# Head means of the delta rule: from one float32 product to two float32r products, with the sums split by ScalarE and VectorE and the products one unit of weights later

## The chip, the core and the metric

The kernel runs on one core of one Trainium2 chip. The metric is the device time of the whole kernel in microseconds (us). One launch computes both layers of the block.

## The reference, cut to what matters

Each of two layers has four mixers side by side. The change touches the end of the first, the gated delta rule:

```python
oa = gated_delta_chunked(qa, ka, va, beta, g).transpose(0, 2, 1, 3)      # 4 heads of 128, 512 tokens
oa = rmsnorm(oa, gdn_norm) * jax.nn.silu(gdn_z.reshape(B, S, GDN_HEADS, GDN_DV).astype(f32))
y_a = oa.reshape(B, S, -1).astype(x.dtype) @ w_br_a
...
g_a, g_b, g_c, g_d = jnp.split(jax.nn.sigmoid(gates), N_BRANCH, axis=-1)
mixed = (g_a * y_a + g_b * y_b + g_c * y_c + g_d * y_d) @ w_o
```

For each head and token, `rmsnorm` needs the mean over the head's 128 values of their squares. The kernel leaves the scale of the queries out of the recurrence, so the epsilon of the norm is multiplied by the queries' own sum of squares, which is added to the squares before the mean is taken.

## The kernel before, in words

Activations lie transposed: 128 channels on the partitions, 512 tokens along the row. A head of the delta rule is one 128x512 tile of `aQ`. Every projection is a job, cut into units of 256 rows of its weight matrix. A job with 512 output columns has 4 output tiles, and a unit of it is 24 products of 128x128 by 128x512: for each of 4 tiles and 2 blocks of rows, high by high, low by high and high by low, since every float32 operand is held as the sum of two float32r tiles (a high part and the low remainder).

The engines run five programs written out by hand. What each waits for is a semaphore count, `upto(name, n)` being the n-th event of that name in the layer. Around the change the programs do this:

- TensorE (`tensor_layer`) multiplies the jobs in a fixed order: `gatea1` (4 units, 1024 rows), `ya0` and `ya1` (2 units each: the output projection of the delta rule), then `cq`, `ck`. The products that take the means, `head_means`, are put between the units of `gatea1`. The tiles of `gatea1` and of `ya0` use the same four banks of PSUM, `big1`, `big2`, `big3`, `big0`: the first product of `ya0` waits until ScalarE has copied tile 0 of `gatea1` out of `big1` (`big_free1`), and until the low parts of heads 0 and 1 are there (`a_olo`, 2 of 4). Its second unit waits for all four.
- ScalarE (`scalar_layer`) squares the heads (`head_squares`), applies Silu to the four `az` tiles, turns the means into reciprocal roots (`head_root`: Ln, then Exp), and rounds the finished heads to their high parts (`o_split`). Only behind the last `o_split` does it copy `gatea1` out of PSUM (`gate_copy`). Silu, and Ln with Exp, are in different tables, and each change of table is an instruction of its own.
- VectorE (`vector_layer`) adds the queries' squares (`query_squares_added`), multiplies a head by its reciprocal root (`head_normed`), multiplies by the norm's weight and the gate (`head_out`), and takes the low part (`o_lo_split`).
- GpSimd rounds the weights of each unit to a high part (`ring_hi`, line 589) and subtracts it for the low part (`ring_lo`, line 592). There are four slots in this ring, and GpSimd starts on a slot when the first product of the next unit says that the slot before is used up.
- SyncE issues the loads of weights into `stage`.

Of the kernel before, what the change touches and what calls it, by code (L numbers as in the profile page):

```python
# [19 lines left out]
ALU = mybir.AluOpType  # L20
ACT = mybir.ActivationFunctionType
AX_X = mybir.AxisListType.X

P = 128
# [257 lines left out]
def mixer_keys():  # L282
# [45 lines left out]
PER_LAYER = {  # L328
    "a_LTm0": 10, "a_LTm1": 10, "a_T0": 4, "a_V": 16, "a_ab": 1, "a_arg": 16, "a_attd": 4, "a_consts": 6,
    "a_dec": 4, "a_decc": 8, "a_ed": 4, "a_g": 2, "a_kbe": 4, "a_ln": 4, "a_lt": 4, "a_lt0": 4, "a_ltc": 4,  # L330
    "a_ltq": 4, "a_nrm": 4, "a_ohi": 4, "a_olo": 4, "a_out": 4, "a_qd": 4, "a_rhi": 2, "a_rs": 4, "a_sc": 3,
    "a_silu": 12, "a_small": 2, "a_smallact": 4, "a_sq": 8, "a_sqlo": 4, "a_tap": 24, "a_z": 4, "an_rs": 4,
    "an_so": 4, "an_sq": 4, "b_clear": 1, "b_exp": 36, "b_fc": 3, "b_fexp": 3, "b_fhi": 3, "b_flo": 3, "b_max": 12,
    "b_nm": 12, "b_ohi": 5, "b_olo": 5, "b_raw": 9, "b_rope": 9, "b_rp": 9, "b_share": 2, "b_sum": 3, "b_zero": 1,
    "b_zinv": 1, "b_zln": 1, "big_done0": 43, "big_done1": 43, "big_done2": 38, "big_done3": 38, "big_free0": 43,
    "big_free1": 43, "big_free2": 38, "big_free3": 38, "c_act": 40, "c_add": 8, "c_bias": 3, "c_exp": 20,
# [14 lines left out]
def hybrid_kernel(nc, ins, out):  # L351
    ctx = ExitStack()
    with ctx:
# [13 lines left out]
        ones_r, rot_r = sb("ones_r", 8, F32R), sb("rot_r", ROT, F32R)  # L367
# [16 lines left out]
        oH, oL = (t[:, :].rearrange("p (k s) -> p k s", s=S) for t in (o_hi, o_lo))  # L384
# [19 lines left out]
        aQ, aK, aV = sview(MB, 4), sview(MB + 2048, 4), sview(MB + 4096, 4)  # L404
# [23 lines left out]
        g_sq, g_rs = sview(S, 2), sview(3 * S, 2)  # L428
# [3 lines left out]
        q_sq = b_raw[:, 5 * S:9 * S].rearrange("p (k w) -> p k w", w=S)  # L432
# [40 lines left out]
        def sem(name):  # L473
            if name not in sems:
                sems[name] = ctx.enter_context(nc.semaphore(name))
            return sems[name]
# [3 lines left out]
        def upto(name, count):  # L480

            return sem(name), count + layer[0] * PER_LAYER.get(name, 0)
# [32 lines left out]
        mix_wait, mix_free, mix_freed = big_wait, big_free, big_freed  # L515
# [13 lines left out]
        def f32(ap):  # L529
            return ap.bitcast(F32)  # L530
# [64 lines left out]
        def scalar_layer(act, l):  # L595
            layer[0] = l
            A = nc.scalar.activation

            def exp_ln_tables():

                nc.scalar.preload_act_table_set("natural_log_exp_and_others")
# [167 lines left out]
            ps = big_wait(act, ("aab", 0))  # L769
# [43 lines left out]
            for b0 in (0, 2):  # L813
                for n in range(1, LEVELS):
                    for e in range(2):
                        ps = mix_wait(act, ("Y", b0 + e, n))
                        if n < LEVELS - 1:
                            i = A(g_Yc[e], ps[:, 0:GH * HB // 2], ACT.Copy)
                        else:
                            i = A(g_Yq[e], ps[HB:P, 0:GH * HB], ACT.Copy)  # L820
# [3 lines left out]
                    for e in range(2) if n == LEVELS - 2 else ():  # L824
                        ps = mix_wait(act, ("V", b0 + e, n))
                        for rows in HALVES:
                            i = A(g_U[e][rows, :, rows], blocks(ps[rows, 0:GH * HB]), ACT.Copy)
# [3 lines left out]
                for b in (b0, b0 + 1):  # L831
# [3 lines left out]
                    ps = mix_wait(act, ("new", b))  # L835
                    mix_free(A(g_Y[b % 2], heads(ps), ACT.Copy), ("new", b))
                    ps = mix_wait(act, ("o", b))
# [3 lines left out]
            for i in range(4):  # L841
                ps = big_wait(act, ("az", i))
# [7 lines left out]
            def head_squares(o, sq, done):  # L850
                A(sq, o, ACT.Square, scale=P ** -0.5).then_inc(sem(done), 1)
# [15 lines left out]
                A(oH[0:rows, i, :], src, ACT.Copy).then_inc(sem(f"{tag}_ohi"), 1)  # L867

            mix_freed(act, ("o", NT - 1))
            head_squares(aQ[:, 0, :], g_sq[:, 0, :], "an_so")  # L870
            head_squares(aQ[:, 1, :], g_sq[:, 1, :], "an_so")
            for i in range(4):
                big_freed(act, ("az", i))
                A(sg[:, 4 + i, :], sg[:, 4 + i, :], ACT.Silu).then_inc(sem("a_z"), 1)
            exp_ln_tables()
            for h in range(4):
                if h < 2:
                    mix_wait(act, ("an", h))
                    head_squares(aQ[:, h + 2, :], g_sq[:, h, :], "an_so")
                else:  # L880
                    act.wait_ge(*upto("a_nrm", h - 1))
                head_root(h, ("an", h), g_rs[:, h % 2, :], "an", EPS * EPS * DK)
                if h == 1:
                    o_split("a", 0, aQ[:, 0, :])
                    o_split("a", 1, aQ[:, 1, :])
# [8 lines left out]
            for i in range(4):  # L894
                ps = big_wait(act, ("cq", i))
                big_free(A(cQ[:, i, :], ps[:, :], ACT.Copy, scale=DH ** -0.5), ("cq", i))
            for i in range(4):
                ps = big_wait(act, ("ck", i))
# [48 lines left out]
            for i in range(4):  # L947
                ps = big_wait(act, ("dqk", i))
# [4 lines left out]
            for i in range(4):  # L953
                ps = big_wait(act, ("dv", i))
                big_free(A(dV[:, i, :], ps[:, :], ACT.Copy), ("dv", i))
            act.wait_ge(*upto("d_rope", 4))
            for i in range(4):
                ps = big_wait(act, ("dg", i))
                big_free(A(dG[:, i, :], ps[:, :], ACT.Silu), ("dg", i))
            exp_ln_tables()  # L960
            for h in range(4):
                ps = mix_wait(act, ("dpv", h))
# [137 lines left out]
            for k in range(KT):  # L1100
                act.wait_ge(*upto("mixed_b", k + 1))
                ps = home((f"yb{k // 4}", k % 4))[0]
# [19 lines left out]
            for g in range(8):  # L1122
# [4 lines left out]
                for i in range(4):  # L1127
                    ps = big_wait(act, (f"up{g}", i))
# [18 lines left out]
        def vector_layer(dve, l):  # L1147
            layer[0] = l
            V = nc.vector
            TT, TS, STT = V.tensor_tensor, V.tensor_scalar, V.scalar_tensor_tensor  # L1150
# [78 lines left out]
                    layer[0] = l  # L1229

            def o_lo_split(tag, i, src, rows=P):
                dve.wait_ge(*upto(f"{tag}_ohi", i + 1))
                TT(oL[0:rows, i, :], src, f32(oH[0:rows, i, :]), ALU.subtract).then_inc(sem(f"{tag}_olo"), 1)

            def gated_last():
# [101 lines left out]
            ps = mix_wait(dve, "ab")  # L1337
# [16 lines left out]
            ps = mix_wait(dve, "gc")  # L1354
            mix_free(V.tensor_copy(s_gc, ps[:, 0:16].rearrange("p (b h) -> p b h", b=4)), "gc")
            mix_freed(dve, "gc")
            ps = mix_wait(dve, "gt")
# [4 lines left out]
            for e in range(2):  # L1362
                rows, low, cols = slice(32 * e, 32 * e + 16), slice(64 + 32 * e, 80 + 32 * e), slice(e * P, (e + 1) * P)
                dve.wait_ge(*upto("a_rhi", e + 1))
                i = TT(g_rows[low, cols], ps[rows, cols], f32(g_rows[rows, cols]), ALU.subtract)
# [141 lines left out]

            def query_squares_added(h):

                dve.wait_ge(*upto("an_so", h + 1))  # L1510
                TT(g_sq[:, h % 2, :], g_sq[:, h % 2, :], q_sq[:, h, :], ALU.add).then_inc(sem("an_sq"), 1)

            for h in range(3):
                query_squares_added(h)
            for h0 in (0, 2):
                for h in (h0, h0 + 1):
                    head_normed(h, aQ[:, h, :], g_rs[:, h % 2, :], "a")
                    if h == 0:
                        query_squares_added(3)
                for h in (h0, h0 + 1):  # L1520
                    dve.wait_ge(*upto("a_z", h + 1))
                    head_out(h, aQ[:, h, :], LGN, sg[:, 4 + h, :], aQ[:, h, :], "a")
                for h in (h0, h0 + 1):
                    o_lo_split("a", h, aQ[:, h, :])
# [217 lines left out]
        def tensor_layer(pe, l):  # L1742
# [45 lines left out]
            def do(name, need=None, between=None):  # L1788

                job = JOB[name]  # L1790
                for i in range(len(job.units)):
                    if need:
                        need(i)
                    unit(job, i)
                    if between:
                        between(i)
# [38 lines left out]
            def done(ins_, key):  # L1835
                ins_.then_inc(sem(home(key)[1]), 1)
# [246 lines left out]
            def head_means(*hs):  # L2083
                for h in hs:
                    ps = tile_of(("an", h))
                    pe.wait_ge(*upto("an_sq", h + 1))
                    done(MM(ps[:, :], f32(ones_r[:, 0:1]).to_broadcast((P, P)), g_sq[:, h % 2, :], start=True, stop=True), ("an", h))

            do("gatea1", between=lambda i: head_means(*((0, 1), (2, 3), (), ())[i]))
            do("ya0", lambda i: pe.wait_ge(*upto("a_olo", 2 * i + 2)))  # L2090
            do("ya1")

# [374 lines left out]
```

## Time and profile before

| What | Value |
|---|---|
| Median of 3 runs | 2280.65 us (2279.39 to 2281.89) |
| The profiled execution's own time | 2280.65 us |
| Its span, first to last instruction | 2278.8 us |
| TensorE busy | 2253.0 us, 99% |
| VectorE, ScalarE, GpSimd busy | 911.3, 733.5, 1301.4 us |
| Mean granted TensorE clock | 0.999 |

The span is what the trace covers. The profiled execution took 1.85 us more than its span. A busy share counts the time between an instruction's start and its modelled end. Products overlap, so a product of 0.39 us can follow the one before after 0.23 us.

### The profile page before, as it was taken

The page shows a single profiled execution, that of the slowest core. Times are in us where ns is not written, and L with a number is a line of the kernel's source. Part 1 is how long each engine was busy: PE and PEld are TensorE (multiplying, and loading weights), DVE is VectorE, ACT ScalarE, POOL GpSimd, SP SyncE. Part 2 cuts the span into 40 slices and gives each one's busy share as a digit, 9 for nine tenths or more (in the row PEclk, how much of TensorE's full clock was granted, in tenths as well). Part 3 has the DMA queues.
Part 4 walks back from the last instruction along what each step waited for, and adds up shares of the span by engine and source line. Part 5 has one row for each costly group of instructions (what it writes and reads, how often), then busy time and mean ns, then how long its engine had stood idle before and what let it go on. Part 6 is the DMA issues. An engine that isn't in the chain of part 4 may idle for free.

```text
span 2278.8 us, 30399 instructions
## 1 busy us (share of the span) xinstructions
PE 2253.0 (99%) x12356; PEld 1835.3 (81%) x12356; DVE 911.3 (40%) x1383; ACT 733.5 (32%) x1455; POOL 1301.4 (57%) x732
## 2 busy tenths in 40 slices
PE   9999999999999999999999999999999999999998
PEld 8788877877877888888887888778778778888887
DVE  4755125234375511122357550443244764102233
ACT  5533135113045411122355340460220544102221
POOL 4623644655564566677655156536556554766774
PEclk9999999999999999999999999999999999999999
DMA  4311321422322232233223123224233223332331
GB/s 152 95 46 47 102 74 56 136 86 84 93 80 70 94 118 94 93 101 93 84 79 95 30 65 102 65 76 119 83 93 94 70 79 102 102 102 93 94 100 65
DMA packets 106667, 199.79 MB, mean 88 GB/s; under 512 B 8800, under 2 KB 19296, under 8 KB 105888
## 3 DMA queue, kind: packets, MB, share of 16 engines
q1 hardware_dynamic: 104608, 188.27, 27.2%
q10 hardware_dynamic: 1920, 9.57, 1.5%
q8 instruction: 99, 1.62, 0.3%
q14 instruction: 40, 0.33, 0.0%
HBM read 192.44 MB, written 2.10 MB: 85 GB/s over the span
## 4 chain that ended last, share of the span: by engine, by line
PE 91%; DVE 4%; ACT 2%; issue 2%; DMA 0%; ACTq 0%; DVEq 0%
PE big L1780 69%; PE mix L1780 10%; PE mix L1942 4%; PE big L2144 1%; PE mix L2112 1%; PE mix L2211 1%; DVE k_lo L1336 1%; PE mix L2123 1%; DVE scr L1323 1%; DVE b_raw L1621 1%; ACT o_hi L626 0%; PE mix L2269 0%; PE mix L1845 0%; PE mix L2255 0%; PE mix L2071 0%
## 5 line engine op out<-in xcount | busy, mean ns | idle before, releaser
L592 POOL TENSOR_TENSOR ring_lo<-stage,ring_hi 128x1024 fp32r<-128x1024 f32 (+3 forms) x364 | 919.3, 2526 | 30.4
L589 POOL TENSOR_SCALAR ring_hi<-stage 128x1024 fp32r<-128x1024 f32 (+3 forms) x364 | 383.6, 1054 | 923.6 <-PE big L1780 842.0
L1780 PE MATMUL big<-h_hi,ring_hi 128*128 128x512 f32 (+1 forms) x1888 | 721.1, 382 | 3.0 <-DVE h_lo L1202 1.2
L1780 PE MATMUL big<-h_lo,ring_hi 128*128 128x512 f32 (+1 forms) x1888 | 708.5, 375 | 0.0
L1780 PE MATMUL big<-h_hi,ring_lo 128*128 128x512 f32 (+1 forms) x1888 | 708.3, 375 | 0.0
L1780 PEld LDWEIGHTS big<-h_hi,ring_hi 128*128 128x128 f32 x1888 | 354.7, 188 | 75.2 <-issue 8.2
L1780 PEld LDWEIGHTS big<-h_lo,ring_hi 128*128 128x128 f32 x1888 | 354.7, 188 | 65.8
L1780 PEld LDWEIGHTS big<-h_hi,ring_lo 128*128 128x128 f32 x1888 | 355.0, 188 | 61.5 <-issue 1.0
L1721 DVE TENSOR_TENSOR h_lo<-scr,h_hi 128x1024 fp32r<-128x1024 f32 x64 | 84.7, 1324 | 248.5 <-ACT h_hi L1120 248.5
L1780 PE MATMUL big<-ring_lo,h_hi 128*128 128x512 f32 x448 | 174.1, 390 | 0.0
L1780 PE MATMUL big<-ring_hi,h_hi 128*128 128x512 f32 x448 | 174.1, 390 | 0.0
L1780 PE MATMUL big<-ring_hi,h_lo 128*128 128x512 f32 x448 | 173.7, 389 | 0.0
L1120 ACT ACTIVATE h_hi<-scr 128x1024 fp32r<-128x1024 f32 x64 | 68.4, 1069 | 262.2 <-PE big L1780 260.2
L1732 DVE SCALAR_TENSOR_TENSOR scr<-big,scr 128x512 f32<-128x512 f32 x64 | 44.3, 692 | 254.5 <-ACT scr L1129 254.0
L1780 PE MATMUL mix<-ring_hi,h_hi 128*128 128x512 f32 x320 | 125.0, 391 | 0.0
L1780 PE MATMUL mix<-ring_hi,h_lo 128*128 128x512 f32 x320 | 124.6, 389 | 0.0
L1780 PE MATMUL mix<-ring_lo,h_hi 128*128 128x512 f32 x320 | 124.5, 389 | 0.0
L1129 ACT ACTIVATE scr<-big 128x512 f32<-128x512 f32 x64 | 38.3, 599 | 262.1 <-PE big L1780 261.2
L1780 PEld LDWEIGHTS big<-ring_hi,h_hi 128*128 128x128 f32 x448 | 84.1, 188 | 18.1 <-issue 0.7
L1780 PEld LDWEIGHTS big<-ring_lo,h_hi 128*128 128x128 f32 x448 | 83.8, 188 | 18.2 <-POOL ring_lo L592 1.0
L1780 PEld LDWEIGHTS big<-ring_hi,h_lo 128*128 128x128 f32 x448 | 84.1, 188 | 17.4
L1780 PE MATMUL big<-o_hi,ring_hi 128*128 128x512 f32 x224 | 88.3, 394 | 1.0 <-ACT scr L684 0.9
(312 smaller groups left out, 2717.0 us busy)
## 6 DMA issues: line engine op xcount, KB each, us to landing
stage<-in_w_in SPq DMA_DIRECT2D x168, 512.0 KB, 3.6
stage<-in_w_mlp_in SPq DMA_DIRECT2D x64, 512.0 KB, 3.6
stage<-in_w_mlp_out SPq DMA_DIRECT2D x64, 512.0 KB, 3.8
stage<-in_w_o SPq DMA_DIRECT2D x16, 512.0 KB, 3.8
stage<-in_w_br_a SPq DMA_DIRECT2D x8, 512.0 KB, 3.8
stage<-in_w_br_c SPq DMA_DIRECT2D x8, 512.0 KB, 3.8
stage<-in_w_br_d SPq DMA_DIRECT2D x8, 512.0 KB, 3.8
stage<-in_w_br_b SPq DMA_DIRECT2D x8, 512.0 KB, 3.5
```

The costliest lines, as they stand in the source:

```text
L589: nc.gpsimd.tensor_scalar(high, w, 1.0, 0.0, ALU.mult, ALU.add).then_inc(sem("w_hi"), 1)
L592: nc.gpsimd.tensor_tensor(low[:, own, :], w[:, own, :], f32(high[:, own, :]), ALU.subtract).then_inc(sem("w_ready"), 1)
L1120: A(hH[:, q:q + 2, :], fT[:, 2 * u:2 * u + 2, :], ACT.Copy).then_inc(sem("f_hi"), 1)
L1129: A(fT[:, 4 * g + i, :], ps[:, :], ACT.Relu).then_inc(sem("f_relu"), 1)
L1323: STT(cv[:, q:], raw[:, 0:S - q], tap(3 - q), cv[:, q:], ALU.mult, ALU.add).then_inc(sem("a_tap"), 1)
L1336: TT(k_sqL[:, i, :], k_sq[:, i, :], f32(k_sqH[:, i, :]), ALU.subtract).then_inc(sem("a_sqlo"), 1)
L1621: TT(t2, t2, bTab[:, S:2 * S], ALU.mult).then_inc(sem("b_rp"), 1)
L1721: TT(hL[:, q:q + 2, :], fT[:, 2 * u:2 * u + 2, :], f32(hH[:, q:q + 2, :]), ALU.subtract).then_inc(sem("f_lo"), 1)
L1732: big_free(STT(fT[:, k, :], ps[:, :], 0.0, fT[:, k, :], ALU.max, ALU.mult), (f"up{g}", i))
L1780: ins_ = MM(o_, a_, r_, start=s0, stop=s1)
L1942: return MM(o_, a_, b_, start=True, stop=True)
L2112: i = MM(c_bank[u][:, at:at + w], hv(cK, h)[:, j * P:(j + 1) * P], hv(cQ, h)[:, j * P:], start=opens, stop=True, skip_group_check=True)
```

## The change

The means of the four heads were one product each: a matrix of ones by the float32 tile of the summed squares. Now each sum is rounded to a high part by ScalarE (`head_sum_high`, into `oH`), VectorE subtracts that for the low part (into `oL`), and the mean is two products by a float32r matrix of ones, accumulated in one bank. ScalarE does the squares of all four heads and the high parts of the first two sums ahead of the Silus, and the high parts of the last two behind them. Before, the squares of heads 2 and 3 stood behind the Silus and waited for the products of heads 0 and 1. TensorE does the products of heads 0 and 1 after the second unit of `gatea1` instead of the first, and those of heads 2 and 3 after the third instead of the second. The counts of `a_ohi` and `an_sq` per layer go from 4 to 8 (that part of the diff is left out).

```diff
@@ scalar_layer
             mix_freed(act, ("o", NT - 1))
-            head_squares(aQ[:, 0, :], g_sq[:, 0, :], "an_so")
-            head_squares(aQ[:, 1, :], g_sq[:, 1, :], "an_so")
+            def head_sum_high(h):
+                act.wait_ge(*upto("an_sq", 2 * h + 1))
+                A(oH[:, h, :], g_sq[:, h % 2, :], ACT.Copy).then_inc(sem("a_ohi"), 1)
+
+            for h in range(2):
+                head_squares(aQ[:, h, :], g_sq[:, h, :], "an_so")
+            for h in range(2):
+                head_sum_high(h)
+            for h in range(2):
+                act.wait_ge(*upto("an_sq", 2 * h + 2))
+                head_squares(aQ[:, h + 2, :], g_sq[:, h, :], "an_so")
             for i in range(4):
                 big_freed(act, ("az", i))
                 A(sg[:, 4 + i, :], sg[:, 4 + i, :], ACT.Silu).then_inc(sem("a_z"), 1)
+            for h in (2, 3):
+                head_sum_high(h)
             exp_ln_tables()
             for h in range(4):
-                if h < 2:
-                    mix_wait(act, ("an", h))
-                    head_squares(aQ[:, h + 2, :], g_sq[:, h, :], "an_so")
-                else:
+                if h >= 2:
                     act.wait_ge(*upto("a_nrm", h - 1))
                 head_root(h, ("an", h), g_rs[:, h % 2, :], "an", EPS * EPS * DK)
                 if h == 1:
@@ vector_layer
             def o_lo_split(tag, i, src, rows=P):
-                dve.wait_ge(*upto(f"{tag}_ohi", i + 1))
+                dve.wait_ge(*upto(f"{tag}_ohi", i + (5 if tag == "a" else 1)))
                 TT(oL[0:rows, i, :], src, f32(oH[0:rows, i, :]), ALU.subtract).then_inc(sem(f"{tag}_olo"), 1)
...
             def query_squares_added(h):
 
+                sums = g_sq[:, h % 2, :]
                 dve.wait_ge(*upto("an_so", h + 1))
-                TT(g_sq[:, h % 2, :], g_sq[:, h % 2, :], q_sq[:, h, :], ALU.add).then_inc(sem("an_sq"), 1)
-
-            for h in range(3):
+                TT(sums, sums, q_sq[:, h, :], ALU.add).then_inc(sem("an_sq"), 1)
+                dve.wait_ge(*upto("a_ohi", h + 1))
+                TT(oL[:, h, :], sums, f32(oH[:, h, :]), ALU.subtract).then_inc(sem("an_sq"), 1)
+
+            for h in range(4):
                 query_squares_added(h)
             for h0 in (0, 2):
                 for h in (h0, h0 + 1):
                     head_normed(h, aQ[:, h, :], g_rs[:, h % 2, :], "a")
-                    if h == 0:
-                        query_squares_added(3)
@@ tensor_layer
             def head_means(*hs):
                 for h in hs:
                     ps = tile_of(("an", h))
-                    pe.wait_ge(*upto("an_sq", h + 1))
-                    done(MM(ps[:, :], f32(ones_r[:, 0:1]).to_broadcast((P, P)), g_sq[:, h % 2, :], start=True, stop=True), ("an", h))
-
-            do("gatea1", between=lambda i: head_means(*((0, 1), (2, 3), (), ())[i]))
+                    pe.wait_ge(*upto("an_sq", 2 * h + 2))
+                    ones = ones_r[:, 0:1].to_broadcast((P, P))
+                    MM(ps[:, :], ones, oH[:, h, :], start=True, stop=False)
+                    done(MM(ps[:, :], ones, oL[:, h, :], start=False, stop=True), ("an", h))
+
+            do("gatea1", between=lambda i: head_means(*((), (0, 1), (2, 3), ())[i]))
             do("ya0", lambda i: pe.wait_ge(*upto("a_olo", 2 * i + 2)))
```

On ScalarE, between the squares of heads 0 and 1 (L851) and the first root (L856 is its Ln, L858 its Exp, L867 an `o_split`), this stands before; the rows L874 are the table of Silu and the four Silus, and L601 is the table of Ln and Exp.

```order
L851 ACTIVATE scr<-scr 128x512
L874 ACT_TABLE_LOAD
L874 ACTIVATE scr<-scr 128x512 [waits big_free1]
L874 ACTIVATE scr<-scr 128x512 [waits big_free2]
L874 ACTIVATE scr<-scr 128x512 [waits big_free3]
L874 ACTIVATE scr<-scr 128x512 [waits big_free0]
L601 ACT_TABLE_LOAD
L851 ACTIVATE scr<-scr 128x512 [waits mix_done3]
L856 ACTIVATE scr<-mix 128x512 [waits mix_done3]
```

And this stands there now (L872 is `head_sum_high`, L883 is the old L874).

```order
L851 ACTIVATE scr<-scr 128x512
L872 ACTIVATE o_hi<-scr 128x512 [waits an_sq] x2
L851 ACTIVATE scr<-scr 128x512 [waits an_sq] x2
L883 ACT_TABLE_LOAD
L883 ACTIVATE scr<-scr 128x512 [waits big_free1]
L883 ACTIVATE scr<-scr 128x512 [waits big_free2]
L883 ACTIVATE scr<-scr 128x512 [waits big_free3]
L883 ACTIVATE scr<-scr 128x512 [waits big_free0]
L872 ACTIVATE o_hi<-scr 128x512 [waits an_sq] x2
L601 ACT_TABLE_LOAD
L856 ACTIVATE scr<-mix 128x512 [waits mix_done3]
```

Six instructions that wait for VectorE (`an_sq`) now stand between the first squares and the table of Ln and Exp, four of them ahead of the Silus; none stood there before.

On VectorE, from the first added squares to the first low parts of the finished heads, before (L1511 adds, L1501 is `head_normed`, L1506 `head_out`, L1233 `o_lo_split`):

```order
L1511 TENSOR_TENSOR scr<-scr,b_raw 128x512 [waits an_so] x3
L1501 TENSOR_TENSOR scr<-scr 128x512 [waits an_rs]
L1511 TENSOR_TENSOR scr<-scr,b_raw 128x512 [waits an_so]
L1501 TENSOR_TENSOR scr<-scr 128x512 [waits an_rs]
L1506 SCALAR_TENSOR_TENSOR scr<-scr,lw 128x512 [waits a_nrm,a_z] x2
L1233 TENSOR_TENSOR o_lo<-scr,o_hi 128x512 [waits a_ohi] x2
```

And now (L1520 adds, L1522 is the low part of a sum, L1509 and L1514 are the old L1501 and L1506):

```order
L1520 TENSOR_TENSOR scr<-scr,b_raw 128x512 [waits an_so]
L1522 TENSOR_TENSOR o_lo<-scr,o_hi 128x512 [waits a_ohi]
L1520 TENSOR_TENSOR scr<-scr,b_raw 128x512 [waits an_so]
L1522 TENSOR_TENSOR o_lo<-scr,o_hi 128x512 [waits a_ohi]
L1520 TENSOR_TENSOR scr<-scr,b_raw 128x512 [waits an_so]
L1522 TENSOR_TENSOR o_lo<-scr,o_hi 128x512 [waits a_ohi]
L1520 TENSOR_TENSOR scr<-scr,b_raw 128x512 [waits an_so]
L1522 TENSOR_TENSOR o_lo<-scr,o_hi 128x512 [waits a_ohi]
L1509 TENSOR_TENSOR scr<-scr 128x512 [waits an_rs] x2
L1514 SCALAR_TENSOR_TENSOR scr<-scr,lw 128x512 [waits a_nrm,a_z] x2
```

Each sum now goes to ScalarE and back before VectorE comes to the next one, and all four are done before the first head is normed.

On TensorE the first products of means are these, before and, in the second block, now. The first stands behind the 24 products of the first unit of `gatea1`, the second behind 48.

```order
L2087 MATMUL mix3<-scr,ones_r 128x512 [waits an_sq,mix_free3]
L2087 MATMUL mix0<-scr,ones_r 128x512 [waits an_sq,mix_free0]
L1780 MATMUL big1<-h_hi,ring_hi 128x512 [waits w_ready]
L1780 MATMUL big1<-h_hi,ring_lo 128x512
L1780 MATMUL big1<-h_lo,ring_hi 128x512
```

```order
L2097 MATMUL mix3<-o_hi,ones_r 128x512 [waits an_sq,mix_free3]
L2098 MATMUL mix3<-o_lo,ones_r 128x512
L2097 MATMUL mix0<-o_hi,ones_r 128x512 [waits an_sq,mix_free0]
L2098 MATMUL mix0<-o_lo,ones_r 128x512
L1789 MATMUL big1<-h_hi,ring_hi 128x512 [waits w_ready]
```

## Rows read from the trace of the kernel before

**Rows 1.** The page: busy time and the granted clock in 40 slices.
```profile
PE 2253.0 (99%) x12356; PEld 1835.3 (81%) x12356; DVE 911.3 (40%) x1383; ACT 733.5 (32%) x1455; POOL 1301.4 (57%) x732
...
PEclk9999999999999999999999999999999999999999
```

**Rows 2.** The chain that ended last, from 202 us: start us, us, what.
```profile
202.36 5.72 PE big L1780 x24
208.09 1.72 PE mix L2087 x4
209.80 5.48 PE big L1780 x24
```

**Rows 3.** Groups by line and shape: count, busy us, mean ns of one, idle before.
```profile
L2087 PE MATMUL mix<-scr,ones_r 128*128 128x512 f32 x16 | 7.5, 592 | 0.0
L2081 PE MATMUL mix<-o_lo,ones_r 128*128 128x512 f32 x8 | 3.2, 398 | 0.0
```

**Rows 4.** TensorE in order of time, start us, us: the first product of `ya0`.
```profile
227.76 0.39 PE L1780 MATMUL big<-o_hi,ring_hi 128*128 128x512 f32 x1
```

**Rows 5.** ScalarE in order of time, layer 0, 203 to 229 us.
```profile
203.54 1.19 ACT L851 ACTIVATE scr<-scr 128x512 f32<-128x512 f32 x2
204.74 1.28 ACT L874 ACT_TABLE_LOAD   x1
206.04 2.19 ACT L874 ACTIVATE scr<-scr 128x512 f32<-128x512 f32 x4
208.25 1.28 ACT L601 ACT_TABLE_LOAD   x1
...
216.49 1.30 ACT L867 ACTIVATE o_hi<-scr 128x512 fp32r<-128x512 f32 x2 [3.50 <-DVE scr L1506]
217.69 0.58 ACT L856 ACTIVATE scr<-mix 128x512 f32<-128x512 f32 x1
...
218.84 0.58 ACT L856 ACTIVATE scr<-mix 128x512 f32<-128x512 f32 x1
219.46 0.63 ACT L858 ACTIVATE scr<-scr 128x512 f32<-128x512 f32 x1
...
224.85 0.63 ACT L867 ACTIVATE o_hi<-scr 128x512 fp32r<-128x512 f32 x1 [0.82 <-DVE scr L1506]
225.39 1.81 ACT L684 ACTIVATE scr<-big 128x512 f32<-128x512 f32 x3
```

**Rows 6.** VectorE in order of time, layer 0, 204 to 217 us.
```profile
204.24 3.44 DVE L1511 TENSOR_TENSOR scr<-scr,b_raw 128x512 f32<-128x512 f32 x2 [1.08 <-ACT scr L851]
210.21 1.58 DVE L1511 TENSOR_TENSOR scr<-scr,b_raw 128x512 f32<-128x512 f32 x1 [2.52 <-ACT scr L851]
...
215.72 1.40 DVE L1506 SCALAR_TENSOR_TENSOR scr<-scr,lw 128x512 f32<-128x512 f32 x2
```

**Rows 7.** Line 1511 alone: durations ns min/median/max, first and last start.
```profile
L1511 DVE TENSOR_TENSOR scr<-scr,b_raw x8: 678/1128/2843, 204.2 to 1344.1; 128x512 f32<-128x512 f32 x8
```

**Rows 8.** GpSimd in order of time, layer 0, 204 to 214 us.
```profile
204.13 2.40 POOL L592 TENSOR_TENSOR ring_lo<-stage,ring_hi 128x1024 fp32r<-128x1024 f32 x1
210.19 1.06 POOL L589 TENSOR_SCALAR ring_hi<-stage 128x1024 fp32r<-128x1024 f32 x1 [3.66 <-PE big L1780]
211.33 2.70 POOL L592 TENSOR_TENSOR ring_lo<-stage,ring_hi 128x1024 fp32r<-128x1024 f32 x1
```

**Rows 9.** ScalarE in order of time, the same place in layer 1.
```profile
1337.88 1.28 ACT L601 ACT_TABLE_LOAD   x1
1346.12 1.30 ACT L867 ACTIVATE o_hi<-scr 128x512 fp32r<-128x512 f32 x2 [3.49 <-DVE scr L1506]
```

**Rows 10.** TensorE in order of time, the kernel's first 10 us.
```profile
1.94 2.77 PE L1885 MATMUL mix<-ones_r 128*128 128x512 f32 x6
...
5.36 2.03 PE L1885 MATMUL mix<-ones_r 128*128 128x512 f32 x8
9.09 0.63 PE L1845 MATMUL big<-consts,scr 128*128 128x128 f32 x4 [1.70 <-ACT scr L641]
```

More of the change, by code:

```diff
@@ L330 @@
     "a_dec": 4, "a_decc": 8, "a_ed": 4, "a_g": 2, "a_kbe": 4, "a_ln": 4, "a_lt": 4, "a_lt0": 4, "a_ltc": 4,
-    "a_ltq": 4, "a_nrm": 4, "a_ohi": 4, "a_olo": 4, "a_out": 4, "a_qd": 4, "a_rhi": 2, "a_rs": 4, "a_sc": 3,
+    "a_ltq": 4, "a_nrm": 4, "a_ohi": 8, "a_olo": 4, "a_out": 4, "a_qd": 4, "a_rhi": 2, "a_rs": 4, "a_sc": 3,
     "a_silu": 12, "a_small": 2, "a_smallact": 4, "a_sq": 8, "a_sqlo": 4, "a_tap": 24, "a_z": 4, "an_rs": 4,
-    "an_so": 4, "an_sq": 4, "b_clear": 1, "b_exp": 36, "b_fc": 3, "b_fexp": 3, "b_fhi": 3, "b_flo": 3, "b_max": 12,
+    "an_so": 4, "an_sq": 8, "b_clear": 1, "b_exp": 36, "b_fc": 3, "b_fexp": 3, "b_fhi": 3, "b_flo": 3, "b_max": 12,
     "b_nm": 12, "b_ohi": 5, "b_olo": 5, "b_raw": 9, "b_rope": 9, "b_rp": 9, "b_share": 2, "b_sum": 3, "b_zero": 1,
```

## The prediction

> **What bounds the kernel now.** I read the page first, then the chain that ended last, then each engine in order of time around the change. TensorE is busy 99% of the span at the full granted clock [rows 1], and the chain around the change is nothing but its products: 24 of a unit of `gatea1` in 5.48 us, 4 passes of the means in 1.72, the next 24 [rows 2]. TensorE does not wait for the delta rule's norm anywhere here. The first product of `ya0` follows the last of `gatea1` at 227.76 us [rows 4]. So the kernel gains what TensorE is spared, and loses whatever reaches TensorE late. What could: `ya0` waits for the low parts of heads 0 and 1, and for ScalarE's first `gate_copy`, which stands behind the last `o_split` in ScalarE's program. That copy ran from 225.39 and took about 0.6 [rows 5], so it was done at 226.0, 1.8 us ahead of the product. This is the whole slack of the place.
>
> **What the products save.** A float32 product of 512 columns is two records, 16 for the 8 means of both layers, of 592 ns [rows 3]; four of them take 1.72 us of the chain [rows 2], 0.43 each. A float32r product with the same ones follows its neighbour at the pace of a gate product, 5.48/24 = 0.228 us; its record (398 ns, line 2081) is like theirs, not like 592 [rows 3]. So a pair of heads costs 4 x 0.228 = 0.91 instead of 1.72: 0.81 less, four pairs, 3.2 us in all.
>
> **The new way to the first product of `ya0`**, on the clock of layer 0, instruction by instruction. Three rules come from rows. A step from one engine to the next costs 0.07. VectorE's operation with two operands in SBUF takes 0.68 alone [rows 7], its successor starting 0.61 after it. But one that begins while GpSimd works stands until GpSimd's instruction has ended, and ends 0.55 later: the first add began at 204.24 with GpSimd's subtraction running from 204.13 to 206.53, and took 2.84; the add at 210.21 met GpSimd's rounding (to 211.25) and took 1.58 [rows 6 to 8]. GpSimd in turn starts 0.3 late (2.70 for 2.40) [rows 8]. It begins 0.55 after the first product of each unit (means end at 209.64; it began at 210.19) and works 3.5 of each 5.5 us.
>
> The Trainium skill (SBUF — State Buffer, "Who interferes with whom") says the same: a VectorE operation with two SBUF inputs and a GpSimd operation that reads SBUF hold a shared port in turn, each for its whole length. By that rule the trace agrees, 2.84 us for 0.68.
>
> TensorE, with nothing late: unit 2 of `gatea1` begins at 207.93 and ends at 213.39; means 0 and 1 to 214.30; third unit to 219.76; means 2 and 3; fourth unit. GpSimd then works 208.5 to 212.3, 214.9 to 218.4, and from 0.55 into the fourth unit.
>
> - Squares 0 and 1 end at 204.73 as before [rows 5]. Add 0 ends at 207.08, as before. High part 0 on ScalarE (0.63) to 207.78, low part 0 to 208.50. Add 1 meets GpSimd's rounding: 210.1. High part 1: 210.80. Low part 1 meets the subtraction: 212.9. Square 2 went in at 210.7; square 3 overwrites sum 1 and waits for low part 1: 213.57. Means 0 and 1 find their parts half a microsecond early.
> - Silus with their table, 1.28 + 2.19 [rows 5]: 217.05. High part 2: 217.63. Low part 2 meets the subtraction: 218.94. Add 3: 219.55. High part 3: 220.25. Low part 3: 220.97. TensorE wants it at 220.2 (mean 3): **a first wait, 0.85 us**. The fourth unit runs 221.50 to 226.96.
> - The table of Ln and Exp starts at 220.25, where it started at 208.25 [rows 5]. Two pairs of Ln and Exp follow (1.15 from Ln to Ln, 1.25 for the last pair) [rows 5]: root 1 at 223.95. The norming of head 1 meets GpSimd's subtraction, till 225.9: 226.47.
> - From here GpSimd is idle, since TensorE stands, and the lengths are those of rows: from the first `head_out` (215.72) to the end of root 3 (220.09) 4.37 us [rows 5, 6]: 226.4 to 230.8. Norm 3, `head_out` 2 and 3, `o_split` 3: its start at 232.9. `gate_copy` 0 starts 0.54 after (224.85 to 225.39) [rows 5] and takes 0.6: 234.06. The first product of `ya0` starts at **234.1**, a wait of 7.1 us. The low parts (229.2, and 234.2 for the second unit) are no longer what it waits for.
>
> Against 227.76 that is 6.35 us late: the saving of 1.6 and waits of 0.85 and 7.1. Layer 1 has the same place at the same distances (table to `o_split` 8.24 us in both) [rows 5, 9]; twice 6.35 is 12.7. Nothing later gives it back: what follows waits for TensorE. GpSimd's ring and its DMAs only start later with TensorE, and have three units of lead.
>
> **The clock after a wait of 7.1 us.** No row of before has TensorE idle so long in the middle. Two rows bound it. At the start, from idle, products of 512 columns came 0.427 us apart (six in 2.77) until 5.36 us, then 0.23; after an idle of 1.70 us they kept the fast pace [rows 10]. The page's clock row shows full speed in both places [rows 1], so the spacing has to be read. 0.427 is 512 columns at 1.2 GHz, and 0.228 is near what 2.4 GHz gives. Some ten products at the slow pace cost 10.4 x 0.2 = 2.1 us; the bounds are nothing and 2.1. 7.1 is much further than 1.70, and I take 2.1 for each layer, 4.2 in all.
>
> The Trainium skill (TensorE: Matmul & The Clock Gate, "What's actually happening") has the clock fall to half after an idle stretch and return only after a busy one. No run here has shown it in mid-kernel yet; with it the sum is the one above, without it 4.2 us less.
>
> **Sum.** 2280.65 (the profiled execution's own time, which is also the median) + 12.7 + 4.2 = 2297.5 us.
>
> **Bounds.** Below: if GpSimd never stood in VectorE's way after add 0, the table would start at 217.5, `ya0` at 229.6, 1.85 late per layer: 2284.3. Above: one more meeting with a subtraction on the way costs 2.84 - 0.68 = 2.2 per layer: 2301.9.
>
> **The rivals.**
>
> - *The wait comes, the clock stays.* For it: the fast pace after 1.70 us idle [rows 10]. Against it: 7.1 is four times that. 2293.4.
> - *VectorE is blocked less than I place it.* The meetings depend on tenths: add 1 wants to start at 208.43, GpSimd at 208.48. Each one missed takes up to 2.2 us off. With all gone, 2284.3; below that price no wait is long enough for the clock.
> - *The way is hidden, and only the saving is left.* It ends on the other side: 2280.65 - 3.2 = 2277.4. The place is the first `gate_copy`. It decides when the copy begins by 225.5, for which the table of Ln and Exp would have to start some 8 us earlier, at 212.2. Add 0 alone is not done before 207.08, and two high parts, square 3 and 3.5 us of Silu and its table make 212.5 without a single visit of VectorE between them; its four visits put 217.5 where GpSimd leaves them alone. I see no way to it unless the program were not bound as I read it.
> - *More blocking,* as in the upper bound: 2301.9 or more.
>
> **How the numbers follow.** My forecast has 0.60, the clock that stays 0.18, less blocking 0.12, the hidden way 0.05, more blocking 0.05. 0.2% is 4.6 us, about what a measurement tells from no change. Slower: 0.60 + 0.18 + 0.05 and half of the 0.12, 0.89. The same: the other half and nearly all of the hidden way, 0.10. Faster by over 4.6 us would take more than the products save: 0.01. The range 2287 to 2303 leaves out the hidden way and most of less blocking. As the likeliest, I name 2297.5.
>
> **What the profile after would show.** Right: passes of the means 0.23 apart; the first table of Ln and Exp near 220.2; an idle of TensorE of some 7 us ahead of `ya0`, ended by the copy of `gatea1`, in both layers; a short one ahead of mean 3; products 0.43 apart behind the long one. Wrong: `ya0` follows `gatea1` without a gap; or the gap is there and is ended by a low part; or the table starts well before 218. If the products of the means were as slow as before, the saving would be missing too.

## The result, and the profile after

| | Median, us | Range | Runs |
|---|---|---|---|
| Before | 2281.06 | 2279.39 to 2281.89 | 4 |
| After | 2297.55 | 2295.77 to 2298.25 | 4 |

The ratio is 1.0071, with a 95% interval of 1.0059 to 1.0084: 16.5 us slower. The profiled execution after has a span of 2296.4 us and a mean granted clock of 0.995 (2278.8 and 0.999 before).

In the table of TensorE's waits (us in total, times, longest us) the waits for `gate_copy` share one line. Before, its four waits were 0.4 us at most:

```profile
PE big L1780 <- ACT scr L684: 1.3, 4, 0.4
```

After, it heads the table:

```profile
PE big L1789 <- ACT scr L684: 15.2, 6, 7.0
PE big L1854 <- ACT scr L641: 3.7, 5, 1.4
...
PE mix L2097 <- DVE o_lo L1522: 0.8, 2, 0.4
```

L684 is `gate_copy`, L1522 the low part of a sum. Of the six waits for L684 after, two are new, one per layer, and they are the long ones. The wait of mean 3 for its low part (L2097) is new as well. TensorE in order of time, after, around the third pair of means and the first products of `ya0` (start us, us; the idle before in brackets):

```profile
220.11 0.40 PE L2097 MATMUL mix<-o_hi,ones_r 128*128 128x512 f32 x1
220.34 0.40 PE L2098 MATMUL mix<-o_lo,ones_r 128*128 128x512 f32 x1
221.15 0.47 PE L2097 MATMUL mix<-o_hi,ones_r 128*128 128x512 f32 x1 [0.41 <-DVE o_lo L1522]
...
234.27 0.76 PE L1789 MATMUL big<-o_hi,ring_hi 128*128 128x512 f32 x1 [6.93 <-ACT scr L684]
234.83 0.63 PE L1789 MATMUL big<-o_hi,ring_lo 128*128 128x512 f32 x1
235.26 0.63 PE L1789 MATMUL big<-o_lo,ring_hi 128*128 128x512 f32 x1
...
237.80 0.39 PE L1789 MATMUL big<-o_lo,ring_hi 128*128 128x512 f32 x1
238.03 0.39 PE L1789 MATMUL big<-o_hi,ring_hi 128*128 128x512 f32 x1
```

The passes of the means are 0.23 us apart, mean 3 waits a little, and `ya0`, which followed without a gap in [rows 4], stands 6.93 us behind its copy. Then its products are 0.43 us apart until 237.80 (0.56 for the first two). Stretches of layers 0 and 1 after (length, busy times, and in the third column from the right TensorE's granted clock) say the same:

```profile
226.00:234.00 8.00, 1.34 (x6) 0.76 (x5) 7.02 (x11) 5.12 (x9) 0.09 (x1) 0.81 0.23 66
234.00:236.00 2.00, 1.73 (x4) 1.47 (x5) 0.37 (x1) 1.98 (x5) 0.80 (x1) 0.50 0.00 0
238.00:240.00 2.00, 2.00 (x10) 1.63 (x9) 0.00 (x0) 2.00 (x2) 0.72 (x1) 1.00 0.21 24
...
1374.00:1376.00 2.00, 2.00 (x6) 1.52 (x5) 0.00 (x0) 1.99 (x2) 2.00 (x1) 0.50 0.00 0
```

0.50 is 1.2 GHz, the lower of the clock's two levels. In layer 1 the wait is 6.96 us, and the slow products last from 1371.8 to 1377.9.

What TensorE waited for is on ScalarE. In order of time, after, layer 0, beside [rows 5]:

```profile
209.47 0.64 ACT L872 ACTIVATE o_hi<-scr 128x512 fp32r<-128x512 f32 x1 [1.36 <-DVE scr L1520]
...
211.57 1.28 ACT L883 ACT_TABLE_LOAD   x1
212.87 2.19 ACT L883 ACTIVATE scr<-scr 128x512 f32<-128x512 f32 x4
...
219.64 0.63 ACT L872 ACTIVATE o_hi<-scr 128x512 fp32r<-128x512 f32 x1 [4.06 <-DVE scr L1520]
220.29 1.28 ACT L601 ACT_TABLE_LOAD   x1
...
232.35 1.29 ACT L867 ACTIVATE o_hi<-scr 128x512 fp32r<-128x512 f32 x2 [1.42 <-DVE scr L1514]
233.55 2.04 ACT L684 ACTIVATE scr<-big 128x512 f32<-128x512 f32 x4
```

The table of Ln and Exp starts 12.0 us later than in [rows 5], and the copy 8.2 us later. ScalarE stood 4.06 us for one of VectorE's adds. VectorE and GpSimd in that time, after:

```profile
208.75 0.68 DVE L1520 TENSOR_TENSOR scr<-scr,b_raw 128x512 f32<-128x512 f32 x1
...
215.62 1.18 DVE L1522 TENSOR_TENSOR o_lo<-scr,o_hi 128x512 fp32r<-128x512 f32 x1 [1.92 <-ACT o_hi L872]
216.72 2.88 DVE L1520 TENSOR_TENSOR scr<-scr,b_raw 128x512 f32<-128x512 f32 x1
```

```profile
208.84 1.51 POOL L589 TENSOR_SCALAR ring_hi<-stage 128x1024 fp32r<-128x1024 f32 x1 [1.95 <-PE big L1789]
...
215.21 1.05 POOL L589 TENSOR_SCALAR ring_hi<-stage 128x1024 fp32r<-128x1024 f32 x1 [2.06 <-PE big L1789]
216.35 2.71 POOL L592 TENSOR_TENSOR ring_lo<-stage,ring_hi 128x1024 fp32r<-128x1024 f32 x1
```

The low part of sum 2 met GpSimd's rounding, the add of sum 3 its subtraction. Each of them ends about half a microsecond behind GpSimd's instruction, as in [rows 6 to 8].

### The profile page after: what moved, and what is told of

Read it like the earlier page. It is cut to its first block, busy times and chain, and to the rows that moved or that the text cites. A ratio compares the mean times of both kernels' runs of the same rounds, so it can differ in the third digit from the quotient of the medians.

```text
span 2296.4 us, 30415 instructions
## 1 busy us (share of the span) xinstructions
PE 2255.5 (98%) x12356; PEld 1838.3 (80%) x12356; DVE 914.6 (40%) x1391; ACT 738.1 (32%) x1463; POOL 1300.9 (57%) x732
## 4 chain that ended last, share of the span: by engine, by line
PE 88%; DVE 5%; ACT 4%; issue 2%; DMA 0%; ACTq 0%; DVEq 0%
PE big L1789 67%; PE mix L1789 10%; PE mix L1951 4%; PE big L2155 1%; PE mix L2123 1%; PE mix L2222 1%; DVE k_lo L1344 1%; PE mix L2134 1%; DVE scr L1520 1%; DVE scr L1331 1%; DVE b_raw L1630 1%; DVE scr L1514 0%; ACT o_hi L626 0%; PE mix L2280 0%; PE mix L1854 0%
```

## The experiments

All times stand against runs of the kernel before on the same chip, whose medians were 2280.4 to 2280.6 us. For each, ratio and interval are given. The changed kernel was timed only for the result above. The medians of before there and here lie within 0.7 us of each other, so a comparison with the changed kernel is good to about 1 us.

### One: the products alone, at the old place

```diff
 # vector_layer
-TT(g_sq[:, h % 2, :], g_sq[:, h % 2, :], q_sq[:, h, :], ALU.add)
+TT(oH[:, h, :], g_sq[:, h % 2, :], q_sq[:, h, :], ALU.add)
 # tensor_layer, head_means of before
-done(MM(ps[:, :], f32(ones_r[:, 0:1]).to_broadcast((P, P)), g_sq[:, h % 2, :], start=True, stop=True), ("an", h))
+ones = ones_r[:, 0:1].to_broadcast((P, P))
+MM(ps[:, :], ones, oH[:, h, :], start=True, stop=False)
+done(MM(ps[:, :], ones, oH[:, h, :], start=False, stop=True), ("an", h))
```

> The kernel before, with one thing of the change alone: each mean is two float32r products at the old place. VectorE's add writes the sum straight into the float32r tile, with no instruction more on ScalarE or VectorE; both products read that same high part, so low parts are left out and the means are doubled. Theory (the saving is 3.2 us, all loss comes from the way of the sums between the engines): passes of the means 0.23 us apart, 0.91 per pair instead of 1.72, no new wait of TensorE, 3.2 us faster than before: near 2277.8, ratio 0.9986. Rival (the products themselves are what costs, by a switch between forms or a slower load of the broadcast ones): passes no closer than 0.43, the ratio at 1.000 or above.

Measured: 2280.02 us, 0.9998 (0.9989 to 1.0007). The products are what they were taken for: the passes at 208.04, 208.27, 208.50 and 208.73 us, 0.23 apart. The time is not. A new wait stands in each layer, 1.05 and 1.09 us (TensorE in order of time, layer 0):

```profile
227.45 0.47 PE L1780 MATMUL big<-o_hi,ring_hi 128*128 128x512 f32 x1 [1.05 <-ACT scr L684]
```

It comes from VectorE, in the same run, against GpSimd:

```profile
221.82 4.33 DVE L1506 SCALAR_TENSOR_TENSOR scr<-scr,lw 128x512 f32<-128x512 f32 x2
```

```profile
221.35 1.47 POOL L589 TENSOR_SCALAR ring_hi<-stage 128x1024 fp32r<-128x1024 f32 x1 [1.20 <-PE big L1780]
222.90 2.71 POOL L592 TENSOR_TENSOR ring_lo<-stage,ring_hi 128x1024 fp32r<-128x1024 f32 x1
```

Two `head_out` operations, 1.40 us where nothing stands against them [rows 6], took 4.33. They met both of GpSimd's instructions, which now come earlier, since they follow TensorE. So the last rounding and the copy came later than before (the copy at 226.73 us for 225.39), and of 1.6 us saved per layer 1.1 went into the wait. The 1.0 us that is left for both layers lies within the interval, which is 2 us wide to either side.

### Two: only the place of the means

```diff
-do("gatea1", between=lambda i: head_means(*((0, 1), (2, 3), (), ())[i]))
+do("gatea1", between=lambda i: head_means(*((), (0, 1), (2, 3), ())[i]))
```

> The kernel before, with float32 products and its own order on ScalarE and VectorE; only the products of the means stand one unit of gatea1 later, as in the change. Theory (the slack at the first copy of gatea1 is 1.8 us, and ScalarE's chain here begins with the wait for the first mean): the squares of head 2 start near 214.5 us instead of 209.54, the copy ends near 230.4, TensorE waits some 2.6 us ahead of ya0 in each layer, no fall of the clock: 2286, range 2284 to 2291. Rival (the later place is harmless and the whole loss is the rounding ahead of and behind the Silus): no wait ahead of ya0, ratio within 0.999 to 1.001.

Measured: 2288.22 us, 1.0032 (1.0020 to 1.0044). TensorE waits 2.31 and 2.30 us for the copy, close to the 2.6 expected, so in the old order, where the squares of head 2 wait for the first mean, the later place alone costs. In the changed kernel they do not wait for it. That the clock would stay was wrong: some 1.7 us per layer went to slow products. TensorE and a stretch of this run:

```profile
230.57 0.47 PE L1780 MATMUL big<-o_hi,ring_hi 128*128 128x512 f32 x1 [2.31 <-ACT scr L684]
...
231.42 0.63 PE L1780 MATMUL big<-o_hi,ring_hi 128*128 128x512 f32 x1
```

```profile
232.00:234.00 2.00, 2.00 (x7) 1.52 (x6) 0.00 (x0) 1.99 (x2) 1.92 (x2) 0.50 0.00 0
```

### Three: the changed kernel, with the copy ahead of the roundings

```diff
                 if h == 1:
+                    gate_copy("a", 1, (0, 1, 2))
                     o_split("a", 0, aQ[:, 0, :])
                     o_split("a", 1, aQ[:, 1, :])
+                    gate_copy("a", 1, (3,))
             o_split("a", 2, aQ[:, 2, :])
             o_split("a", 3, aQ[:, 3, :])
-            gate_copy("a", 1)
```

> The changed kernel, with one thing moved: ScalarE copies tiles 0 to 2 of gatea1 ahead of the rounding of heads 0 and 1, and tile 3 right behind it, instead of all four behind head 3. Theory (the 7 us wait is the copy's place behind the last rounding): the first product of ya0 then waits for the low part of head 1, near 229.4, so 2.2 us instead of 7; GpSimd starts again with it and blocks VectorE, so the second unit of ya0 waits some 2.4 us for head 3; no stretch of slow products if the clock needs a longer idle; 2288, range 2285 to 2291. If the clock falls after 2.2 us as well, 2291 to 2293. Rival (the wait is one for the low parts, whatever the copy does): 2297.5 as the changed kernel, the first product near 234.3.

Measured: 2288.53 us, 1.0035 (1.0022 to 1.0049), 9 us less than the changed kernel. In each layer the long wait is gone, and what is left is one for a low part:

```profile
228.76 0.50 PE L1790 MATMUL big<-o_hi,ring_hi 128*128 128x512 f32 x1 [2.11 <-DVE o_lo L1242]
...
236.57 0.50 PE L1790 MATMUL big<-o_hi,ring_hi 128*128 128x512 f32 x1 [0.43 <-DVE o_lo L1242]
```

The rival is out: it was the copy. The median met its number, but by two errors against each other. The wait at the second unit was 0.43 instead of 2.4, because the unit ahead of it ran some of its products at 1.2 GHz (from 230.25 to 233.2, 0.43 us apart), which I had not expected after 2.1 us. At the full pace the unit would have ended 1.6 us earlier and the wait would have been longer by as much. So what the slow products took here would have been waiting otherwise, and the 2291 to 2293 us expected for a fall of the clock did not come.

### Four: products that keep TensorE busy

```diff
+            mix_freed(pe, ("an", 0))
+            spun(28)
             do("ya0", lambda i: pe.wait_ge(*upto("a_olo", 2 * i + 2)))
```

> The changed kernel, with 28 products of ones by ones added behind gatea1 in each layer, into a bank that nobody reads any more, so that TensorE is busy for some 6.2 of the 7 us in which it waited. They compute nothing that is used. Theory (the idle itself makes the clock fall to 1.2 GHz and costs 1.5 us in layer 0 and 2.8 in layer 1): the first product of ya0 at the same place, behind it products 0.23 us apart, the granted clock 1.00, 4.3 us faster than the changed kernel: 2293.2. Rival (the slow products come from something else at that place, such as reading fresh float32r tiles or new weights): the same slow stretch, 2297.5.

Measured: 2292.73 us, 1.0055 (1.0040 to 1.0071), 4.8 us less than the changed kernel. The first product of `ya0` starts 30.36 us after ScalarE's first squares (203.45), in the changed kernel 30.37, so its place is the same, and behind it the pace is full. TensorE in order of time:

```profile
226.67 6.28 PE L1894 MATMUL mix<-ones_r 128*128 128x512 f32 x28
...
233.81 0.47 PE L1789 MATMUL big<-o_hi,ring_hi 128*128 128x512 f32 x1 [0.85 <-ACT scr L684]
234.11 0.40 PE L1789 MATMUL big<-o_hi,ring_lo 128*128 128x512 f32 x1
234.35 0.40 PE L1789 MATMUL big<-o_lo,ring_hi 128*128 128x512 f32 x1
```

Same data, same weights, same operations, with 0.85 us of idle ahead of them in place of 6.93: without the long idle the clock stays.

### Five: the Silus out of the way

```diff
 # ahead of the last two blocks of the delta rule
+nc.scalar.preload_act_table_set("silu_and_others")
...
-big_free(A(sg[:, 4 + i, :], ps[:, :], ACT.Copy), ("az", i))
+big_free(A(sg[:, 4 + i, :], ps[:, :], ACT.Silu), ("az", i))
...
-for i in range(4):
-    big_freed(act, ("az", i))
-    A(sg[:, 4 + i, :], sg[:, 4 + i, :], ACT.Silu).then_inc(sem("a_z"), 1)
```

> The changed kernel, with the Silus taken out of the way: their table is loaded while ScalarE still waits in the last blocks of the delta rule, and the four copies of az out of PSUM are Silus themselves, so the table and four operations (3.5 us) are gone from between the high parts. Theory (the wait is the length of ScalarE's and VectorE's way to the first copy of gatea1): the table of Ln and Exp starts near 216.5 instead of 220.3, no wait ahead of mean 3, the copy ends near 229.6, and TensorE waits 2.8 us ahead of ya0 instead of 7. Per layer -1.6 for the products, +2.8, and +1.7 for the slow stretch of the clock that followed waits of 2.1 and 2.3 us: 2286, range 2282 to 2290. Rival (the Silus only filled time in which ScalarE waits for VectorE's adds): the same 2297.5.

VectorE's `head_out` waits for these Silus instead of the ones taken out (left out above).

Measured: 2288.46 us, 1.0037 (1.0024 to 1.0049), 9 us less than the changed kernel. The table of Ln and Exp starts at 215.83, 4.5 us earlier. TensorE's wait is 3.56 us, not 2.8:

```profile
229.69 0.76 PE L1788 MATMUL big<-o_hi,ring_hi 128*128 128x512 f32 x1 [3.56 <-ACT scr L684]
```

The two low parts of heads 0 and 1 took 4.23 us against GpSimd on the way. The rival is out: the Silus did not only fill time in which ScalarE waited for VectorE.

### Six and eight: the same, with the copy moved too

Six moves tiles 0 to 2 of the copy ahead of the rounding of heads 2 and 3, eight all four:

```diff
+            gate_copy("a", 1, (0, 1, 2))      # eight: all four tiles here
             o_split("a", 2, aQ[:, 2, :])
             o_split("a", 3, aQ[:, 3, :])
-            gate_copy("a", 1)
+            gate_copy("a", 1, (3,))           # eight: nothing here
```

> The kernel of the run above, and ScalarE copies tiles 0 to 2 of gatea1 ahead of the rounding of heads 2 and 3, tile 3 behind it. Computes all that the reference asks. Theory (with every wait gone the kernel keeps the 3.2 us of the products): no wait of TensorE over 0.4 us between gatea1 and ya1, full clock, 2277.5, ratio 0.9986 with an interval below 1. Rival (the products' gain is lost again wherever the first wait goes, as 1.1 us came back per layer in the run with the products alone): 2279 to 2281, a wait for a low part of heads 0 to 3 at one of ya0's units.

Measured: 2285.01 us, 1.0020 (1.0011 to 1.0029). A miss, and above the rival's 2279 to 2281 too. ScalarE in order of time shows tile 3 behind a rounding that waited 2.17 us for VectorE, and TensorE waited 2.23 us for it in each layer, with slow products behind the wait:

```profile
231.31 0.63 ACT L869 ACTIVATE o_hi<-scr 128x512 fp32r<-128x512 f32 x1 [2.17 <-DVE scr L1514]
231.85 0.58 ACT L684 ACTIVATE scr<-big 128x512 f32<-128x512 f32 x1
```

> The kernel with Silu from PSUM, and all four copies of gatea1 ahead of the rounding of heads 2 and 3 (the run before this left tile 3 behind it). Computes all that the reference asks. Theory (in that run the wait of 2.2 us, and the slow products after it, came from tile 3's copy, which stood behind a rounding that had waited for VectorE at two of GpSimd's instructions): the copy of tile 3 ends near 227.9, no wait for it; the low part of head 3 near 232.7 against 232.2 makes a wait of 0.5 us at the second unit of ya0 per layer, no slow products: 2278.4, range 2277 to 2280, ratio 0.9990. Rival (the low part of head 3 comes much later than that, since VectorE is where the time goes): a wait of 1.5 to 3 us at the second unit and 2281 to 2285.

Measured: 2280.56 us, 1.0000 (0.9991 to 1.0009). The wait for the copy is gone and the clock stays (1.00 in the stretch from 232 to 236 us), but the wait for head 3's low part is 1.10 us, 1.15 in layer 1, not 0.5, and the median lies above the range of 2277 to 2280:

```profile
232.94 0.50 PE L1788 MATMUL big<-o_hi,ring_hi 128*128 128x512 f32 x1 [1.10 <-DVE o_lo L1240]
```

So with the copy's wait gone the change is worth nothing against the kernel before: of the 3.2 us that the products save, 2.3 go into this wait, and the rest lies within the interval. `head_out` of heads 2 and 3, which leads to that low part, starts at 227.15 us here and at 221.65 in seven, and takes 4.34 us in both; what is late is the way to it.

### Seven: the products at the old place, with the copy moved

The edit of one, and `gate_copy` as in six.

> The kernel before with the two float32r products per mean at the old place, as in the first run (low parts left out, means doubled), and ScalarE copies tiles 0 to 2 of gatea1 ahead of the rounding of heads 2 and 3, tile 3 behind it. Theory (in the first run 1.1 us per layer of the 1.6 saved came back as a wait for the copy, since TensorE's earlier units moved GpSimd's work onto VectorE's last operations): no wait at ya0, 3.2 us faster than before: 2277.3, ratio 0.9986. Rival (it was not the copy): the wait of 1.1 us stays, or stands at a low part, and the ratio stays at 0.9998.

Measured: 2277.47 us, 0.9988 (0.9979 to 0.9997), 3.1 us faster than before against 3.2 expected; by the interval it could be 0.7 to 4.8. There is no wait between `gatea1` and `ya0`. As in one, the low parts are left out and the means are doubled.

### Nine: one rounded product

```diff
 # on top of seven
-MM(ps[:, :], ones, oH[:, h, :], start=True, stop=False)
-done(MM(ps[:, :], ones, oH[:, h, :], start=False, stop=True), ("an", h))
+done(MM(ps[:, :], ones, oH[:, h, :], start=True, stop=True), ("an", h))
```

> The kernel before with one float32r product per mean at the old place, VectorE's add writing the rounded sum straight into the float32r tile, and ScalarE copying tiles 0 to 2 of gatea1 ahead of the rounding of heads 2 and 3. The low parts of the sums are left out, so the means are those of sums rounded to float32r; everything else is as the reference asks. Theory (eight products of 0.43 x 2 each become eight of 0.23, and no wait comes up): 8 x (0.86 - 0.23) = 5.0 us faster than before, 2275.5, ratio 0.9978. Rival (TensorE reaches ya0 0.9 us earlier still, GpSimd's work moves onto VectorE's last operations, and a wait for the copy or a low part takes 1 us or more per layer back): 2277.5 or above.

Measured: 2276.25 us, 0.9983 (0.9974 to 0.9992), 4.3 us faster than before (5.0 expected) and 21 faster than the changed kernel. It gives up the low parts of the four sums, and with them all that carried them between the engines.

## Why the prediction was right, point by point

The prediction had 16.9 us from before to after, and 16.5 were measured. That the two times agree to 0.05 us is chance: the sum began at 2280.65, and the median of before beside the result is 2281.06.

**The product's saving** was 3.2 us: passes 0.23 us apart in the changed kernel, and 3.1 us where nothing takes it back (seven, interval 0.7 to 4.8). The spacing is the firmer of the two.

**The slack of 1.8 us at the copy, and the wait that follows** were the heart of it. The first product of `ya0` was put at 234.1 and came at 234.27, the wait at 7.1 and was 6.93. Three shows that it is the copy's place that makes it so long, and five that it shortens with ScalarE's way. Measured from ScalarE's first squares to the first product of `ya0`, layer 0 went from 24.22 to 30.37 us (before 203.54 and 227.76, after 203.90 and 234.27): 6.15 late, where the prediction had 6.35. Layer 1 was 6.13 late.

**The way there** was right at its end and wrong in the middle. Add 1 was to meet GpSimd's rounding and end at 210.1. VectorE took its add up at 208.75, 0.09 us before GpSimd began (208.84), and GpSimd was the one to be late (1.51 us for 1.05). The table of Silu thus started at 211.57, not 213.57. The 2 us were lost again at once: the low part of sum 2 and the add of sum 3 met GpSimd in turn (1.18 and 2.88), where the prediction had one meeting. The table of Ln and Exp started at 220.29, put at 220.25. So the rule of who waits for whom held each time, while the order of two starts a tenth apart could not be told in advance. That the sum came out so near is in this part luck. Some 2 us per layer were at stake; without them the sum would have been 2293.5, still within the range. That GpSimd is what held VectorE up rests on these ends in the traces; no run took GpSimd's work away.

**The wait ahead of mean 3** was put at 0.85 us. The second pass of mean 2 and the first of mean 3 are 0.81 apart, where 0.23 is the pace: 0.6.

**The clock** was put at 2.1 us a layer, for a fall that no row of before showed in mid-kernel. It fell in both. Layer 0: eight gaps in 3.53 us (234.27 to 237.80), which are 1.8 at the full pace: 1.7 lost. Layer 1: fourteen gaps in 6.06 us (1371.82 to 1377.88), 3.2 at the full pace: 2.9 lost. Together 4.6 for 4.2, and layer 1 lies above the 2.1 that the prediction took for the upper bound of a layer. Four shows that the idle is the cause. The 12.3 us by which the two layers' first products are late and the 4.6 us of slow products make 16.9 us; the medians differ by 16.5. So the prediction put the first products 0.4 us too late in all and the clock 0.4 us too cheap, and the two errors cancel.

**The rivals.** The clock that stays, the hidden way and more blocking are out by the traces. Less blocking happened at one place and was made up at the next. Its price of 2284.3 was too low: with `ya0` 1.85 us late TensorE would have waited some 3.4 us, and five shows slow products after 3.56, 1.5 us per layer. By an estimate from these numbers this rival, and the lower bound with it, belonged near 2287.3.

## What to carry to other kernels

When one engine is busy 99% of the time, ask of a change first what it does to the slack of the others, and only then what it saves on that engine. Here 3.2 us of products were bought with eight trips between ScalarE and VectorE, four per layer, and the place had 1.8 us to spare. A wait of the busy engine is best looked for at the buffers that come free late, such as a copy that stands behind unrelated work, and not only at the data it needs. And a saving on the busy engine moves everything that follows it: in one, GpSimd's work came earlier, fell on VectorE's last operations, and two thirds of the saving were gone until the copy was moved as well.

## What the runs showed of the hardware that I had not expected

TensorE's clock fell to 1.2 GHz after much shorter idles than 7 us. In the middle of the kernel, idles of 0.85 us (four), of 1.05 to 1.15 (one, eight) and of 1.44 (twice in the kernel before) left it at full speed. Idles of 2.1 (three), 2.2 (six), 2.3 (two), 3.6 (five) and 6.9 us were followed by products 0.43 us apart, in both layers. But the length of the idle does not decide alone. At the kernel's start 1.70 us [rows 10] had kept the clock, and in five so did 2.22 us: the six products of 512 columns behind it took 1.56 us in all, which is the full pace.

```profile
8.88 1.18 PE L1853 MATMUL big<-consts,scr 128*128 128x128 f32 x8 [2.22 <-ACT scr L641]
9.81 1.56 PE L1893 MATMUL mix<-ones_r 128*128 128x512 f32 x6
```

No run here separates what else decides.

The slow pace does not always begin with the first product. In layer 0 of two, TensorE took up its work at 230.57 and the slow pace began at 231.42; in layer 1, after the same 2.3 us, it was there at once. How much longer the slow stretch takes than the full pace would is not set by the idle either: 1.7 us in both layers of two, three and six, 1.5 in both of five, and 1.7 and 2.9 after two idles of the same 6.9 us. A wait of 2.3 us on this engine thus cost 4.0 in two, where both layers together lost 7.8.

A change of tables on ScalarE took 1.28 us, with 0.02 us ahead of it and 0.02 behind (219.64, 220.29 and then 221.59 us in the changed kernel). Counted from start to start that is 1.95 us between two operations that without it stand 0.53 apart (209.47 and 210.00), so a change cost 1.4 us. The Trainium skill (ScalarE: Activation LUTs, "What ACT_TABLE_LOAD costs") adds a drain to each switch, for some 2.66 us in all; the trace does not show one here.
